# Depthwise convolution beside a stream of matmuls: low parts of weights made by GpSimd, running sums in PSUM, no plain fp32 units

## The reference

```python
def _conformer_layer(x, norm_g, w_in, dw_w, dw_b, ln_g, ln_b, w_out):
    h = _rms_norm(x, norm_g)
    u = h @ w_in                           # 256x2048 by 2048x6144
    a, b, z = jnp.split(u, 3, axis=-1)
    y = a * jax.nn.sigmoid(b)
    y = _depthwise_causal_conv(y, dw_w, dw_b)   # 31 taps per channel, 2048 channels
    y = jax.nn.silu(_layer_norm(y, ln_g, ln_b))
    y = y * jax.nn.silu(z)
    return x + y @ w_out
```

## Time and profile before

| | |
|---|---|
| median of 3 runs | 1283.67 us (1282.76 to 1283.9) |
| the profiled execution | 1284.22 us, span of its profile 1281.7 us |
| TensorE busy | 1273.0 us, 99% |
| VectorE, ScalarE, GpSimd busy | 834.1, 791.9, 38.4 us |
| DMA | 248 MB, mean 194 GB/s |

### The profile page before, as it was taken

How to read it: one execution, slowest core, us unless ns; L and a number is a source line. 1 busy time by engine, 2 the same in 40 slices (tenths; PEclk the granted TensorE clock), 3 DMA queues, 4 the chain that set the end, 5 groups by cost and what they waited for, 6 DMA issues and landing times.

```text
span 1281.7 us, 16175 instructions
## 1 busy us (share of the span) xinstructions
PE 1273.0 (99%) x5993; PEld 1052.5 (82%) x5993; DVE 834.1 (65%) x1259; ACT 791.9 (62%) x1293; POOL 38.4 (3%) x86
## 2 busy tenths in 40 slices
PE   9999999999999999999999999999999999999998
PEld 8877777778888888888888888889988888888886
DVE  5689999988657665445666675555644445566545
ACT  6699999966547554445466665446744445666543
POOL 1011111100000000000000000000000000000000
PEclk9999999999999999999999999999999999999999
DMA  9699999965656656665544545566655556655564
GB/s 297 214 247 266 282 273 290 263 202 165 190 187 183 189 187 186 195 194 185 177 150 149 160 152 183 184 188 163 187 167 154 154 162 183 196 166 162 181 196 133
DMA packets 134277, 248.06 MB, mean 194 GB/s; under 512 B 12060, under 2 KB 22936, under 8 KB 134040
## 3 DMA queue, kind: packets, MB, share of 16 engines
q1 hardware_dynamic: 128840, 227.63, 56.9%
q0 software_dynamic: 5328, 19.40, 7.9%
q10 hardware_dynamic: 32, 0.01, 0.0%
HBM read 225.51 MB, written 2.10 MB: 178 GB/s over the span
## 4 chain that ended last, share of the span: by engine, by line
PE 93%; ACT 3%; DVE 1%; DMA 1%; issue 1%; DVEq 0%; ACTq 0%
PE PS L1522 27%; PE PS L1524 27%; PE PS L1523 27%; PE PS L1445 3%; PE PS L1456 2%; ACT tap_products L948 2%; PE PS L1510 2%; DMA w_raw<-in_a_w_in 1%; ACT w_hi L524 1%; PE PS L1545 0%; PE PS L1546 0%; PE PS L1544 0%; DVE w_lo L985 0%; ACT L505 0%; PE PS L1583 0%
## 5 line engine op out<-in xcount | busy, mean ns | idle before, releaser
L985 DVE TENSOR_TENSOR w_lo<-w_raw,w_hi 128x1024 fp32r<-128x1024 f32 (+1 forms) x409 | 496.6, 1215 | 365.1 <-ACT w_hi L524 363.7
L524 ACT ACTIVATE w_hi<-w_raw 128x1024 fp32r<-128x1024 f32 (+1 forms) x409 | 428.9, 1051 | 375.3 <-PE PS L1524 356.7
L1522 PE MATMUL PS<-w_hi,actA_hi 128*128 128x512 f32 x844 | 334.5, 396 | 0.2
L1524 PE MATMUL PS<-w_hi,actA_lo 128*128 128x512 f32 x844 | 329.0, 390 | 0.0
L1523 PE MATMUL PS<-w_lo,actA_hi 128*128 128x512 f32 x844 | 328.5, 389 | 0.0
L1522 PE MATMUL PS<-w_hi,actB_hi 128*128 128x512 f32 (+1 forms) x768 | 304.8, 397 | 0.0
L1524 PE MATMUL PS<-w_hi,actB_lo 128*128 128x512 f32 (+1 forms) x768 | 297.2, 387 | 0.0
L1523 PE MATMUL PS<-w_lo,actB_hi 128*128 128x512 f32 (+1 forms) x768 | 296.5, 386 | 0.0
L1522 PEld LDWEIGHTS PS<-w_hi,actA_hi 128*128 128x128 f32 x844 | 158.5, 188 | 35.2 <-issue 3.1
L1523 PEld LDWEIGHTS PS<-w_lo,actA_hi 128*128 128x128 f32 x844 | 158.6, 188 | 33.6 <-issue 1.9
L1524 PEld LDWEIGHTS PS<-w_hi,actA_lo 128*128 128x128 f32 x844 | 158.4, 188 | 33.4
(11 more groups left out here) (253 smaller groups left out, 840.8 us busy)
## 6 DMA issues: line engine op xcount, KB each, us to landing
w_raw<-in_a_w_in SPq DMA_DIRECT2D x96, 512.0 KB, 6.8
w_raw<-in_w_in SPq DMA_DIRECT2D x88, 512.0 KB, 3.7
w_raw<-in_w_kv SPq DMA_DIRECT2D x64, 512.0 KB, 4.0
w_raw<-in_b_w_in SPq DMA_DIRECT2D x64, 512.0 KB, 3.8
tap_products<-tap_products POOLq DMA_DIRECT2D x37, 512.0 KB, 7.9
w_raw<-in_a_w_out SPq DMA_DIRECT2D x32, 512.0 KB, 4.1
w_raw<-in_b_w_out SPq DMA_DIRECT2D x32, 512.0 KB, 3.8
w_raw<-in_w_out SPq DMA_DIRECT2D x32, 512.0 KB, 4.2
```

The source lines that it names most:

```text
L524: nc.scalar.activation(split_slot(u)[0], w_raw[:, RAW_SLOT[u], 0:2 * w], ACT.Copy)\
L985: V.tensor_tensor(wl, w_raw[:, RAW_SLOT[u], 0:2 * w], wh.bitcast(F32), ALU.subtract)\
L1522: T.matmul(bank, ah, wh[:, kk, :], start=first and kk == 0, stop=False)
L1524: ins = T.matmul(bank, al, wh[:, kk, :], start=False, stop=last and kk == 1)
```

## The change

- GpSimd makes the low parts of units 18 to 91 (74 units); VectorE makes the others, as before. `LO_READY` names for each unit the semaphore that tells of it. GpSimd does the subtractions and the issues of the pair sums in the order of the steps.
- High and low parts have five slots for units 15 to 104 (the two new ones in space that `x_t` had and other free space). From unit 18 on the split comes earlier, and from unit 20 on it stands four steps ahead of the unit, and not two (`SPLIT_AT`).
- No unit is plain. `whole_parts` and `x_t` are gone.
- The running sums of a group are in PSUM banks 6 and 7 (`tap_sums`). The last solo tap (kind "last") writes to `conv` in SBUF. The groups follow each other, none is mixed with the next. A group's solo taps number 19, 19, 19 and 17.
- 25 pairs: 6, 6, 6 and 7. A pair's two taps can stand in different steps. The planner's leads and costs are other ones.
- The statistics' transposes use banks 4 and 5, and so wait for copies of y (`t_copied`), and y and z transposes wait for `stats_read`. `STATS_AT` becomes 40, 55, 71, 87; the normalisation is at 89, 90, 96, 99 (before 92, 93, 99, 102); z's transposes are at 93, 96, 101, 103 (before 93, 96, 100, 103).

The planned steps change thus. Before, the taps, adds and pairs of a group are spread over 20 units or more. After, group 1 has its 76 tap operations in steps 36 to 47 and 51 (20 of them, the last four of group 0 among these, in step 36), with adds in 36, 40, 43, 45, 47, 49 and 51; group 2 the like from 51; group 3 from 67, with its last pair made in steps 79 and 81 and its last add and last tap in step 86.

```diff
+PARTS_WIDE, WIDE_SPLIT = 5, range(15, 105)
+PART_SLOT = [u % (PARTS_WIDE if u in WIDE_SPLIT else PARTS) for u in range(NU)]
+PART_PREV = [max([v for v in range(max(0, u - 10), u) if PART_SLOT[v] == PART_SLOT[u]], default=None) for u in range(NU)]
+SPLIT_AT = [v - AHEAD - min((max(v - WIDE_SPLIT[PARTS - 1], 0) + 1) // 2, PARTS_WIDE - PARTS) * (v in WIDE_SPLIT) for v in range(NU + PARTS_WIDE)]
...
-PLAIN = {21, 35, 46, 53, 55, 64, 76, 82, 87, 89}
-PAIRS, SUMS, ADDENDS = [9, 10, 9, 9], 5, 3
+POOL_FROM, POOL_TO = 18, 92
+LO_BY_POOL = [POOL_FROM <= u < POOL_TO for u in range(NU)]
+LO_READY = [("w_lo_pool" if LO_BY_POOL[u] else "w_lo_ready", LO_BY_POOL[:u + 1].count(LO_BY_POOL[u])) for u in range(NU)]
+PAIRS, SUMS, ADDENDS = [6, 6, 6, 7], 5, 3
...
-ACT_LEAD, DVE_LEAD, PAIR_LAG = 0, -5, 4
+ACT_LEAD, DVE_LEAD, PAIR_LAG = -15, 30, 5
...
+        def tap_sums(i, n=1):
+            return PS[:, 6 + i // 2, i % 2 * SEQ:(i % 2 + n) * SEQ]
...
-            for n in range(PAIR_FROM[4]):
-                pool.wait_ge(S["products_ready"], n + 1)
-                chain.dma_start(pair_products(n, 0), pair_products(n, 1), accum_op=ALU.add)\
-                    .then_inc(S[f"pair{n % SUMS}_summed"], 16)
+            for u in range(SPLIT_AT[POOL_FROM], CONV_TO):
+                for v in splits_at(u):
+                    if LO_BY_POOL[v]:
+                        w_part, w_rest = split_slot(v)
+                        pool.wait_ge(S["w_hi_ready"], v + 1)
+                        chain.tensor_tensor(w_rest, w_raw[:, RAW_SLOT[v], :], w_part.bitcast(F32), ALU.subtract)\
+                            .then_inc(S["w_lo_pool"], 1)
+                for j, m in [(j, m) for j, m, half in PAIRS_AT.get(u, []) if half]:
+                    n = PAIR_FROM[j] + m
+                    pool.wait_ge(S["products_ready"], n + 1)
+                    chain.dma_start(pair_products(n, 0), pair_products(n, 1), accum_op=ALU.add)\
+                        .then_inc(S[f"pair{n % SUMS}_summed"], 16)
...
-                        ins = V.tensor_scalar(conv[:, k, :], y_pad[:, k, 0:SEQ], taps[:, k, 0:1],
+                        if j:
+                            name, value = tap_done[k - 4]
+                            dve.wait_ge(S[name], value)
+                        ins = V.tensor_scalar(tap_sums(i), y_pad[:, k, 0:SEQ], taps[:, k, 0:1],
                                               gain("a_dw_b", k), ALU.mult, ALU.add)
-                    elif kind == "tap":
+                    elif kind in ("tap", "last"):
                         dve.wait_ge(S[tap_done[k][0]], tap_done[k][1])
-                        ins = V.scalar_tensor_tensor(conv[:, k, :], y_pad[:, k, tap:tap + SEQ],
-                                                     taps[:, k, tap:tap + 1], conv[:, k, :],
-                                                     ALU.mult, ALU.add)
+                        ins = V.scalar_tensor_tensor(tap_sums(i) if kind == "tap" else conv[:, k, :],
+                                                     y_pad[:, k, tap:tap + SEQ], taps[:, k, tap:tap + 1],
+                                                     tap_sums(i), ALU.mult, ALU.add)
...
-                        ins = V.tensor_tensor(conv[:, k:k + 2, :], conv[:, k:k + 2, :],
-                                              pair_products(n, 0)[:, i:i + 2, :], ALU.add)
+                        ins = V.tensor_tensor(tap_sums(i, 2), tap_sums(i, 2),
+                                              pair_products(n, 0)[:, i:i + 2, :].rearrange("p a b -> p (a b)"),
+                                              ALU.add)
```

More of the change, by code:

```diff
@@ L118, in plan_convolution @@
     act_at = dve_at = pe_at = 0
-    made, added, taken = [], 0, [0] * 4
+    made, halves, added, taken = [], 0, 0, [0] * 4
     for u in range(CONV_FROM[0], CONV_TO):
@@ L136, in plan_convolution @@
                 continue
-            open_taps = [i for i in range(4) if u >= CONV_FROM[i]
-                         and taken[i] < len(SOLO_TAPS[i]) - (added < PAIR_FROM[i + 1])]
-            if not open_taps:
+            j = len(STATS_AT)
+            if u < CONV_FROM[j] or taken[j] == len(SOLO_TAPS[j]) - (added < PAIR_FROM[j + 1]):
                 break
-            j = open_taps[0]
-            CONV_OPS[u] += [(j, "tap" if taken[j] else "first", SOLO_TAPS[j][taken[j]], k) for k in range(4)]
+            kind = "first" if not taken[j] else "tap" if taken[j] + 1 < len(SOLO_TAPS[j]) else "last"
+            CONV_OPS[u] += [(j, kind, SOLO_TAPS[j][taken[j]], k) for k in range(4)]
             dve_at, taken[j] = dve_at + 16, taken[j] + 1
@@ L153 @@
 Z_EVAC_AT = [73, 80, 89, 96]
-Z_AT = [93, 96, 100, 103]
+Z_AT = [93, 96, 101, 103]
 ROPE_AT = FIRST[C_V] + 6
[L156 to L161, removed]
 DIFF_FROM, DIFF_STEP = FIRST[C_ZB] - 8, 5
@@ L982, in split @@
                     return
[L983 removed]
+                dve.wait_ge(S["w_hi_ready"], u + 1)
                 wh, wl = split_slot(u)
@@ L1502, in products @@
                 first, last = i == 0, i == len(kts) // 2 - 1
[L1503 to L1524, removed]
+                name_lo, n_lo = LO_READY[u]
+                pe.wait_ge(S[name_lo], n_lo)
+                wh, wl = (part.rearrange("p (k n) -> p k n", k=2) for part in split_slot(u))
+                for kk in range(2):
+                    k = k_first + kts[2 * i + kk]
+                    for tok in toks:
+                        ah = hi[which][:, k, tok * P:(tok + 1) * P]
+                        al = lo[which][:, k, tok * P:(tok + 1) * P]
+                        bank = chunk_bank(c, tok)
+                        T.matmul(bank, ah, wh[:, kk, :], start=first and kk == 0, stop=False)
+                        T.matmul(bank, ah, wl[:, kk, :], start=False, stop=False)
+                        ins = T.matmul(bank, al, wh[:, kk, :], start=False, stop=last and kk == 1)
                 if TT - 1 in toks:
@@ L1618, in _ @@
                     pe.wait_ge(S["y_ready"], j + 1)
+                    if any(at < u for at in STATS_AT):
+                        pe.wait_ge(S["stats_read"], 2 * sum(1 for at in STATS_AT if at < u))
                     transpose_chunk(f"y{j}", staged(1))
@@ L1622, in _ @@
                         pe.wait_ge(S["conv_ready"], j + 1)
+                        pe.wait_ge(S["t_copied"], sum(1 for m in range(4) if 16 * m + 18 <= u))
                         if j:
                             pe.wait_ge(S["stats_read"], 2 * j)
-                        else:
-                            pe.wait_ge(S["tables_ready"], 1)
                         for tok in range(TT):
                             for i in range(4):
-                                ins = T.transpose(PS[:, 6 + tok, i * P:(i + 1) * P],
+                                ins = T.transpose(PS[:, 4 + tok, i * P:(i + 1) * P],
                                                   conv[:, 4 * j + i, tok * P:(tok + 1) * P], ident[:, :])
```

101 lines of the change are left out of this document (51 added, 50 removed).

## The result

The changed kernel takes 1303.62 us in the median of four runs, against 1283.29 for the kernel before on the same chip: a ratio of 1.0158, with a 95% interval of 1.014 to 1.0176. It is 1.6% slower, where 0.6% faster was forecast, and the time lies above the range of 1274.5 to 1286 us. The profiled execution has a span of 1301.8 us.

A forecast was written before the change was run, and what follows sets the result against it. TensorE, busy 99%, was taken as the bound. On the profiled span 1281.7 - 7.2 - 1.2 + 0.3 + 0.6 = 1274.2 us; plus 2.5 less 0.5 gave 1276.2 us, range 1274.5 to 1286.

The forecast's parts named there:

- Two engines and one port: VectorE's y products, two SBUF inputs, may wait for a running GpSimd subtraction; 0.6 us charged for all four.
- the sigmoid was to be done at 58.7 us: Step 16: two ScalarE splits before staging y move the sigmoid from 57.7 to 58.7 us; margin 0.9 us.
- the sum: Likeliest case, all terms added: 1274.2 us span, 1276.2 us time, own range 1274.8 to 1279; chance 0.74.
- The plain units: Ten plain fp32 units on TensorE become split units, 3.44 to 2.72 us each: 7.2 us less, the main term.
- GpSimd's subtraction: 74 subtractions of 128x1024 on GpSimd: 2.3 us each, bounds 1.7 and 2.7; it keeps up until 2.50 us.
- The taps in PSUM: VectorE's taps with running sums in PSUM: 0.40 us each, no difference from SBUF; upper end 0.46.
- rival B: VectorE late because PSUM taps cost 0.46 us: stalls of 5.0 us before y products, 1280.3 us; chance 0.06.
- A group of 16 units: Per group TensorE needs 45.3 us; VectorE 39.8, ScalarE 40.5, GpSimd 42.0 and DMA transfers 41.2 fit within it.
- The last statistics: TensorE's 1.2 us wait before the last LayerNorm statistics' transposes goes, 0.3 given back; last tap at 15.7 against 16.3 us.
- Bunched taps: VectorE's work bunched at each group's start; y slack 1.3 us in group 1, 2.6 in group 2.
- C: GpSimd's subtraction just too slow, 2.57 to 2.72 us: 7.4 us come back, 1282.7, no change; chance 0.06.
- D: GpSimd becomes the bound before units 18 to 91, subtractions waiting for VectorE taps at the port: 1307 us; chance 0.14.

The follow-up runs named there:

- the sigmoid's version: Changed kernel, but ScalarE writes the sigmoid in PSUM and VectorE's y product reads it there, with one SBUF input: 1277.77 us, ratio 0.9956.
- the busy wait: Changed kernel, but TensorE does 24 unneeded 128x128 matmuls ahead of the y transposes of groups 1 to 3: 1296.33 us, ratio 1.0103.
- the best version: Changed kernel with sigmoid in PSUM, y staged before step 16's two splits, GpSimd waiting for LayerNorm's diagonals in step 87: 1277.40 us, ratio 0.9954.

## Why the prediction was wrong

**The step that failed** is "Two engines and one port", the term of 0.6 us. The mechanism was named there: the product may have to wait for a running subtraction, "up to 2.3 us more". It was priced as one remainder of one subtraction, and at the first y it was no more: the product took 2.04 us. At the other three it took 8.8 to 9.4 us, waiting until GpSimd's row of work ended, and TensorE waited 5.7 to 6.3 us each time, 18.8 us with the first. I had reasoned from slack (1.3 us at a product) and from the length of one instruction, and never asked whether there is a moment between two. With the pair issues in the same queue and no wait behind them, these three times there was none.

The rest of a subtraction is 0.8 of the 1.1 us at the first y. The same paragraph has another slip: the sigmoid was to be done at 58.7 us and was done at 59.8, as ScalarE waited for loads (0.84, 0.26 and 0.33 us) that were said not to be late. In the sigmoid's version it is done at 60.7, and TensorE waits 1.3 us though nothing holds the product.

**Its second half**: no term for the clock. A wait of 6 us was not in the sum, so what TensorE does after it wasn't either: another 7.3 us, by the busy wait. 18.2 (18.8 less the 0.6) and 7.3 are 25.5 of the 27.4 us by which the forecast missed; the sigmoid's version, which has 1.3 us of the one and nothing of the other, is 25.9 us faster than the changed kernel.

**The plain units** were worth less than 7.2 us. From the y at 60.61 us to the y at 200.69 the kernel before has six of them and takes 140.08 us; the best version takes 136.13 (60.57 to 196.70). That is 3.95 us, 0.66 each and 6.6 for ten. The rest of the miss is this 0.6 and about 1.3 us that I can't place.

**What held.** GpSimd's subtraction: 2.37 us start to start, against 2.3 taken between bounds of 1.7 and 2.7. GPSIMD Engine Reference of the Trainium skill (Performance versus the Vector engine) gave the same estimate, and the trace agrees. The taps in PSUM: 477 ns against 476, so rival B is out. The 65 ns more that VectorE: DVE Perf Modes of the Trainium skill (the TRN2 errata) gives for a PSUM source are not seen here. A group of 16 units: 45.7 us for 45.3 forecast, VectorE in it 39.7 for 39.8, ScalarE 38.8 for 40.5, GpSimd 43.9 for 42.0, DMA share 0.95, all in the sigmoid's version. The last statistics: no wait. It was tighter than the prediction's sum said: its own terms (2.7, 3.2 and 7.9) make 13.8 us and not 12.9, and so 16.6 for the last tap against 16.3. Bunched taps didn't delay a product: in the changed kernel VectorE was idle for 2.2 to 4.6 us before each, waiting for ScalarE's sigmoid. The sigmoid's version, in which only the failed step is taken away, is at 1277.8 where the sum said 1276.2.

**The rivals.** B, C and D were all something else than what happened. D had the right place for the contention (the port) and the wrong victim: it let GpSimd's subtractions wait for VectorE, and it was VectorE that waited, in an operation with a deadline. With the sums in SBUF both waited. SBUF — State Buffer of the Trainium skill (the shared port pair) says that whichever starts first holds the pair for its instruction and the other one fully blocks. The runs agree where subtractions end cleanly (2.4 us and less for the product with a wait behind each subtraction or each issue); in the changed kernel the hold went on over four subtractions.

## What to carry to other kernels

When work moves to GpSimd, list every remaining VectorE operation with two SBUF inputs and give each a PSUM input, or a moment in which GpSimd is quiet; four left over cost 25.9 us here, where the change without them gains 5.4. A wait on a shared resource is priced by the row of the other's work that can stand without a break, not by one instruction; and a head start for the other engine can make that row longer. And a wait of TensorE of several microseconds is dearer than its length, since it goes on at the lower clock.

## What was not expected of the hardware

- Subtractions of 128x1024 on GpSimd last 2.4 us, but up to 4.2 us after several pair issues with no wait between, while their starts stay 2.37 us apart. A wait on one of them behind each issue brings them back to 2.4 to 2.7 us.
- VectorE operations with one SBUF tensor can be held too when their output is in SBUF: a tensor_scalar of 128x2 took 2.14 us in the changed kernel and 0.17 us in the best version, where GpSimd is quiet. With the sums in SBUF the first operation of a sum took 2.7 us; with its output in PSUM it took 0.54 us beside the same subtractions.

```profile
L1280 DVE TENSOR_SCALAR st<-st 128x2 f32<-128x2 f32 x1 | 2.1, 2143 | 0.0
...
L1285 DVE TENSOR_SCALAR st<-st 128x2 f32<-128x2 f32 x1 | 0.2, 170 | 0.0
```

- The first operation of a sum, a tensor_scalar of 128x256 from SBUF, has a mean of 407 ns into SBUF (before) and 539 ns into PSUM, while the taps take the same time in both.
